# Delta rule loop: two steps a turn with buffers by parity, the late level first, and level copies shared by bank

## The reference

```python
m = jnp.einsum('bhnid,bhnjd->bhnij', kb, k) * dec_strict      # gram product, decayed
a = m + jnp.eye(CHUNK)
u = triangular_solve(a, v * beta)                             # the inverse of a is needed
w = triangular_solve(a, kb * exp(gam))
qk = jnp.einsum('bhnid,bhnjd->bhnij', q, k) * dec_incl
def step(s, xs):                                              # from chunk to chunk
    v_new = u_c - w_c @ s
    o = qd_c @ s + qk_c @ v_new
    s = gl_c * s + kd_c.T @ v_new
```

## Time and profile before

| | |
|---|---|
| median of 3 runs | 3768.53 us (3765.59 to 3772.26) |
| profiled execution, its own time | 3773.59 us |
| its span | 3771.8 us |
| mean granted clock of TensorE | 0.935 |
| PE, PEld | 3270.4 us (87%), 2736.9 us (73%) |
| DVE, ACT, POOL | 1995.1 (53%), 1669.3 (44%), 1715.4 (45%) |
| delta rule stage | about 1062 to 1702 us of the span |

### The profile page before, as it was taken

The page is one execution under the profiler, slowest core; times in us unless marked ns, Lnnn a source line. Parts: engine busy times, 40 slices in busy tenths (PEclk is TensorE's granted clock), DMA queues, the critical chain, the costliest instruction groups (busy, mean ns, idle before and its releaser), DMA issues. The chain is left out here.

```text
span 3771.8 us, 114554 instructions
## 1 busy us (share of the span) xinstructions
PE 3270.4 (87%) x49145; PEld 2736.9 (73%) x49145; DVE 1995.1 (53%) x2896; ACT 1669.3 (44%) x2453; POOL 1715.4 (45%) x1364
## 2 busy tenths in 40 slices
PE   6899999999968788775677566999999999999998
PEld 3677888888857777764666535878877887787877
DVE  5488510111025555555666667665565546657575
ACT  5566422442135565552444424564454453323243
POOL 0211222333035555532666337546646656656564
PEclk8899999999979999995877867999999999999999
DMA  5133443353233333324433365766675666645453
GB/s 199 48 68 73 101 101 95 107 139 114 70 99 112 112 114 113 109 86 116 114 103 91 134 211 183 234 228 197 199 249 173 204 204 248 245 161 220 177 223 123
DMA packets 438348, 555.94 MB, mean 147 GB/s; under 512 B 119788, under 2 KB 355664, under 8 KB 413656
## 3 DMA queue, kind: packets, MB, share of 16 engines
q1 hardware_dynamic: 411936, 514.10, 42.7%
q10 hardware_dynamic: 20536, 21.58, 1.7%
q0 software_dynamic: 5632, 16.78, 1.5%
HBM read 354.42 MB, written 197.97 MB: 146 GB/s over the span
## 5 line engine op out<-in xcount | busy, mean ns | idle before, releaser
L3015 PE MATMUL o_pg<-o_t_hi,o_s_hi 128*128 128x512 f32 x2016 | 793.4, 394 | 47.1 <-ACT o_part L3062 13.0
L3017 PE MATMUL o_pg<-o_t_lo,o_s_hi 128*128 128x512 f32 x2016 | 790.2, 392 | 0.0
L3018 PE MATMUL o_pg<-o_t_hi,o_s_lo 128*128 128x512 f32 x2016 | 789.9, 392 | 0.0
L600 PE MATMUL p_pg<-h_hi,p_whi 128*128 128x512 f32 (+1 forms) x1384 | 531.6, 384 | 9.5 <-DVE p_wlo L827 9.5
L600 PE MATMUL p_pg<-h_lo,p_whi 128*128 128x512 f32 (+1 forms) x1384 | 519.4, 375 | 0.0
L600 PE MATMUL p_pg<-h_hi,p_wlo 128*128 128x512 f32 (+1 forms) x1384 | 519.3, 375 | 0.0
L3015 PEld LDWEIGHTS o_pg<-o_t_hi,o_s_hi 128*128 128x128 f32 x2016 | 381.8, 189 | 137.7 <-DVE o_s_lo L3222 35.7
L3018 PEld LDWEIGHTS o_pg<-o_t_hi,o_s_lo 128*128 128x128 f32 x2016 | 381.9, 189 | 80.1
L3017 PEld LDWEIGHTS o_pg<-o_t_lo,o_s_hi 128*128 128x128 f32 x2016 | 381.7, 189 | 78.7
L3222 DVE TENSOR_TENSOR o_s_lo<-o_raw,o_s_hi 128x512 fp32r<-128x512 f32 x288 | 267.5, 931 | 202.6 <-ACT o_s_hi L3051 202.6
L600 PEld LDWEIGHTS p_pg<-h_hi,p_whi 128*128 128x128 f32 x1384 | 262.4, 190 | 61.0 <-DVE p_wlo L827 9.8
(11 more groups left out here) (334 smaller groups left out, 6669.3 us busy)
## 6 DMA issues: line engine op xcount, KB each, us to landing
o_raw<-in_w_mlp SPq DMA_DIRECT2D x32, 1024.0 KB, 6.4
scr_f<-o_xf SPq DMA_DIRECT2D x64, 512.0 KB, 8.1
o_raw<-scr_f SPq DMA_DIRECT2D x32, 1024.0 KB, 5.3
scr_w<-o_pre SPq DMA_DIRECT2D x16, 1792.0 KB, 7.1
o_t_raw<-scr_w SPq DMA_DIRECT2D x28, 1024.0 KB, 4.9
g_kqvb<-scr_kqv SPq DMA_DIRECT2D x72, 384.0 KB, 3.5
o_xf<-scr_x SPq DMA_DIRECT2D x22, 1024.0 KB, 7.7
p_raw<-in_w_in SPq DMA_DIRECT2D x38, 512.0 KB, 5.8
```

The lines of the kernel that those rows point to most:

```text
L600: last = nc.tensor.matmul(pg[0:m, bank, 0:n], w[:, q, k, 0:m], h[bank][:, k, :], start=(k == 0 and j == 0), stop=(k == KT - 1 and j == 2))
L3015: nc.tensor.matmul(out, s_hi[:, q, k, :], t_hi[:, q, k, :], start=(not more and k == 0), stop=False, skip_group_check=more)
L3017: nc.tensor.matmul(out, s_hi[:, q, k, :], t_lo[:, q, k, :], start=False, stop=False, skip_group_check=more)
L3018: last = nc.tensor.matmul(out, s_lo[:, q, k, :], t_hi[:, q, k, :], start=False, stop=(k == 3), skip_group_check=more)
```

## The change

- `steps`: body 0 and body 1 written out, a loop of 16 turns with bodies 2 and 3, then bodies 34, 35 and 36 written out. `at`, `chunks` and the column slices count two steps a turn.
- `nn`, `tt`, `am` and `kqvb` are pairs of buffers, chosen by the parity of the chunk. The copies `hand_nn`, `hand_tt`, `keep_inverse` and `vtake` go, with `nn2`, `tt2`, `ttb` and `vt`. `residual_end` reads the turned values from PSUM.
- `take(l)` on ACT copies bank 0 alone; a new `take_rest(l)` on DVE copies bank 1; PE waits for both.
- The order within a body changes on PE, ACT, DVE and POOL; SP loads the rows of gamma two chunks ahead and `kqvb` first.

The core of the diff:

```diff
-    return n0 * per + c if i is None else i * per + (n0 * per + c)
+    return n0 * per + c if i is None else i * (2 * per) + (n0 * per + c)
...
-        nn, nn2, tt, tt2, ttb, am, amb = (sb("g_" + n, [P, *W]) for n in ("nn", "nn2", "tt", "tt2", "ttb", "am", "amb"))
+        nn, tt, am = ([sb(f"g_{n}{p}", [P, *W]) for p in range(2)] for n in ("nn", "tt", "am"))
+        amb = sb("g_amb", [P, *W])
...
             body(None, 0, True, False, True)
-            with eng.Fori(0, NCH - 2) as i:
-                body(i, 1, True, True, True)
+            body(None, 1, True, True, True)
+            with eng.Fori(0, (NCH - 4) // 2) as i:
+                body(i, 2, True, True, True)
+                body(i, 3, True, True, True)
+            body(None, NCH - 2, True, True, True)
             body(None, NCH - 1, True, True, False)
...
                 def body(i, n, a, c, pre):          # SP
+                    if a:
+                        if i is not None or n > 1:
+                            sp.wait_ge(qs_done, at(i, n, 1, -1))
+                        load_kqvb(i, n)
                     if pre:
-                        sp.wait_ge(d_ready, at(i, n, 1, 1))
-                        load_rows(i, n + 1)
+                        if i is not None or n < NCH - 2:
+                            sp.wait_ge(d_ready, at(i, n, 1, 2))
+                            load_rows(i, n + 2)
                         sp.wait_ge(kkq_done, at(i, n, 1, 1))
                         load_kqa(i, n + 1)
-                    if a:
-                        if c:
-                            sp.wait_ge(qs_done, at(i, n, 1, 0))
-                        load_kqvb(i, n)
...
                     def grown(l):
                         pe.wait_ge(tx_ready, at(i, n, 3, l + 1))
+                        pe.wait_ge(tx_rest, at(i, n, 3, l + 1))
...
                     def ks():
+                        pe.wait_ge(kqvb_in, at(i, m, 32, 32))
+                        pe.wait_ge(s_ready, at(i, m, 1, 1))
                         pe.wait_ge(o_ready, at(i, m, 1, 1))
...
                     def qs():
-                        pe.wait_ge(vt_ready, at(i, m, 1, 1))
+                        pe.wait_ge(z_ready, at(i, m, 1, 1))
...
                     def take(l):                    # ACT
                         act.wait_ge(tx_done, at(i, n, 3, l + 1))
-                        nc.scalar.activation(txs[:, :, :, :, :], pa[:, :, :, :, :], ACT.Copy).then_inc(tx_ready, 1)
+                        nc.scalar.activation(txs[:, 0], pa[:, 0], ACT.Copy).then_inc(tx_ready, 1)
...
+                    def take_rest(l):               # DVE
+                        dve.wait_ge(tx_done, at(i, n, 3, l + 1))
+                        dve.tensor_copy(txs[:, 1], pa[:, 1]).then_inc(tx_rest, 1)
...
                     def decay():
-                        if c:
-                            dve.wait_ge(tt2_ready, at(i, n, 1, 0))
+                        if i is not None or n > 1:
+                            dve.wait_ge(tz_done, at(i, n, 1, -1))
...
                     def residual_end():
                         dve.wait_ge(z_half, at(i, m, 1, 1))
-                        dve.wait_ge(vt_ready, at(i, m, 1, 1))
-                        dve.tensor_tensor(z[:, :, :, :], z[:, :, :, :], vt[:, :, :, :], ALU.subtract).then_inc(z_ready, 1)
+                        dve.wait_ge(kv_turned, at(i, m, 1, 1))
+                        dve.tensor_tensor(heads_first(z), heads_first(z), pd[:, :, 1], ALU.subtract).then_inc(z_ready, 1)
```

More of the change, by code:

```diff
@@ L945, in phase_gdn @@
         glq = sb("g_glq", [P, NCH, 2 * PAIRS])
-        kqa, kqvb = sb("g_kqa", [P, 2, 2, PAIRS, CH]), sb("g_kqvb", [P, 2, 3, PAIRS, CH])
+        kqa = sb("g_kqa", [P, 2, 2, PAIRS, CH])
+        kqvb = [sb(f"g_kqvb{p}", [P, 2, 3, PAIRS, CH]) for p in range(2)]
         grow = sb("g_grow", [P, *W])
@@ L1031, in load_kqvb @@
                         src = e.skqv[:, ds(chunks(i, n)[g], 1)]
-                        sp.dma_start(kqvb[:, g].rearrange("p (c j) a t -> p c (j a t)", c=1),
+                        sp.dma_start(kqvb[n % 2][:, g].rearrange("p (c j) a t -> p c (j a t)", c=1),
                                      src.rearrange("p c j t -> p c (j t)")).then_inc(kqvb_in, 16)
@@ L1191, in product @@
                         pe.sem_inc(go, 1)
-                        turn(side(pa, 1), tile(tt))
-                        to_channels(side(pa, 0), tile(nn), tile(tt)).then_inc(tx_done, 1)
+                        turn(side(pa, 1), tile(tt[p]))
+                        to_channels(side(pa, 0), tile(nn[p]), tile(tt[p])).then_inc(tx_done, 1)
                     def grown(l):
                         pe.wait_ge(tx_ready, at(i, n, 3, l + 1))
+                        pe.wait_ge(tx_rest, at(i, n, 3, l + 1))
                         pe.sem_inc(go, 1)
@@ L1203, in late_product @@
                         pe.wait_ge(pred2_done, at(i, m, 3, l - 2))
-                        pe.wait_ge(nn2_ready, at(i, m, 1, 1))
                         pe.sem_inc(go, 1)
-                        turn(side(pc, 1), tile(tt2))
-                        to_channels(side(pc, 0), tile(nn2), tile(tt2)).then_inc(tx2_done, 1)
+                        turn(side(pc, 1), tile(tt[q]))
+                        to_channels(side(pc, 0), tile(nn[q]), tile(tt[q])).then_inc(tx2_done, 1)
                     def late_grown(l):
@@ L1253, in amvn @@
                         back(side(pb, 0), tile(amb), tile(vn)).then_inc(amvn_done, 1)
+                    if c:
+                        late_grown(2)
                     if a:
@@ L1257, in body @@
                     if c:
-                        kv()
-                        late_grown(2)
-                        late_product(3)
+                        late_product(3)
+                        ks()
+                        kv()
+                        late_grown(3)
                     if a:
                         product(0)
-                    if c:
[L1264 to L1267, removed]
                     if c:
@@ L1271, in body @@
                     if a:
-                        product(1)
+                        grown(0)
                     if c:
@@ L1275, in body @@
                     if a:
-                        grown(1)
+                        product(1)
                     if c:
@@ L1279, in body @@
                     if a:
+                        grown(1)
+                    if c:
+                        kdvn()
+                    if a:
                         product(2)
                     if c:
-                        kdvn()
                         amvn()
@@ L1333, in keep_am @@
                             act.wait_ge(amvn_done, at(i, m, 1, 0))
[L1334 to L1356, removed]
+                        src = am[m % 2]
+                        nc.scalar.activation(amb[:, :, 0:2, :], src[:, :, 0:2, :], ACT.Copy)
+                        nc.scalar.activation(amb[halves(1), :, 2:4, :], src[halves(0), :, 2:4, :], ACT.Copy)
+                        nc.scalar.activation(amb[halves(0), :, 2:4, :], src[halves(1), :, 2:4, :], ACT.Copy).then_inc(amb_ready, 1)
                     def vntake():
@@ L1388, in gaps @@
                 def gaps(i, n):
-                    nc.gpsimd.tensor_copy(cola[:, :, :, :].unsqueeze(2), colq[:, 0:3, ds(i + n if i is not None else n, 1)])\
+                    nc.gpsimd.tensor_copy(cola[:, :, :, :].unsqueeze(2), colq[:, 0:3, ds(i * 2 + n if i is not None else n, 1)])\
                         .then_inc(cola_ready, 1)
@@ L1407, in take_colb @@
                 def take_colb(i, n):
-                    st = i + n if i is not None else n
+                    st = i * 2 + n if i is not None else n
                     nc.gpsimd.tensor_copy(colb[:, :, :, :].unsqueeze(2), colq[:, Q_KDEC:Q_REST, ds(st, 1)])
@@ L1422, in body @@
                     m = n - 1
+                    if pre:
+                        gaps(i, n + 1)
+                    if a:
+                        pool.wait_ge(tt_half, at(i, n, 1, 1))
+                        pool.wait_ge(c_ready, at(i, n, 1, 1))
+                        nc.gpsimd.tensor_tensor(tt[n % 2][:, :, :, :], tt[n % 2][:, :, :, :], c2[:, :, :, :], ALU.add).then_inc(tt_init, 1)
+                    if pre:
+                        pool.wait_ge(tt_init, at(i, n, 1, 1))
+                        seeds(i, n + 1)
                     if c:
@@ L1533, in body @@
                     if a:
+                        decay()
                         attend()
                     if c:
+                        residual()
+                        late_block(3)
+                    if a:
+                        take_rest(0)
+                    if c:
                         keys()
-                        late_block(3)
-                        residual()
+                        residual_end()
                     if a:
@@ L1541, in body @@
                     if c:
-                        residual_end()
+                        late_block(4)
                         carried()
```

(3 more changed lines are left out.)

79 lines of the change are left out of this document (30 added, 49 removed).

## The result

The changed kernel takes 4170.0 us (median of four executions), against 3770.4 us for the one before: a ratio of 1.105, 95% interval 1.102 to 1.108. The profiled execution took 4175.8 us, its span is 4174.0 us.

What follows compares the result with a forecast made beforehand. No engine was full; the two-step body's code loading on PE was to set the pace. Sixteen turns of 859 us plus 50 us for two written-out steps replace 563.1: +346 us, 4115 us, range 3965 to 4290.

Steps and rivals of the forecast that it cites:

- The mechanism: Delta rule loop on PE: the two-step body does not stay and is loaded again every turn; chance 0.80.
- The pace: PE's code loading in the delta rule loop: one block every 4.13 us, averaged over eight intervals between stalls.
- Blocks of a turn: PE's two-step loop body: 13 blocks loaded a turn, 53.7 us, sixteen turns 859 us.
- The two steps newly written out: Steps 1 and 34 on PE run first-time code: 25 us each, 50 us together.
- The jump: PE's loop end: the jump back may wait behind an unneeded load; in the upper bound, 14 blocks at 4.6 us.
- The most that any row shows PE to keep is 8 blocks: PE's code: 8 blocks loaded for the present loop, against 12.4 for the two-step body, taken as not staying.
- The new order: PE's queue in a delta rule step: reordering and sharing worth 0 to 0.3 us a step, nothing under the load pace.
- SyncE and POOL ... both ends zero: Gamma rows loaded a step ahead and POOL's distances first: PE waits for neither queue, so zero gain.
- set at what it was: residual_end on DVE, reading PSUM instead of vt: its time taken as unchanged.
- the order pays: Rival: code stays, three copies each reach PE 0.42 us sooner, 1.26 us a step, 3748 us; chance 0.11.

Runs made afterwards that it cites:

- e1: The kernel before with a turn of two steps and nothing else changed: 4133.2 us, ratio 1.096.
- e3: The changed kernel with PE's 37 bodies written out and no jump on PE, other engines keeping their loops: 4050.5 us, ratio 1.074.
- e8: The kernel before with the first half of each gram product computed ten times, a body of 8.5 blocks: 4456 us in one execution.
- e10: The kernel before with the first half of each gram product computed three times, a body of 6.7 blocks: 4049 us in one execution.
- e11: The kernel before with the first half of each gram product computed twice, a body of 6.45 blocks: 3779 us in one execution.
- e2: The changed kernel with one step a turn, its handover between buffers left out so only the time counts: 3754.2 us, ratio 0.995.
- e5: The changed kernel with one step a turn, ScalarE's two handover copies back, single am and kqvb: 3760.4 us, ratio 0.997.
- e6: e5 with the three level copies whole on ScalarE, none shared: 3756.1 us, ratio 0.996.
- e7: The kernel before with the three level copies shared by bank, old order, one step a turn: 3765.7 us, ratio 0.997.

## Why the prediction was right

*The mechanism* was right: the two-step body is loaded in every turn, e1 shows it alone. Forecast 400 blocks, 408 measured.

*The pace* of 4.13 us a block, read from eight stalls of code that ran first, was right: 4.11. That it agrees so closely is in part luck, for the pace isn't one number: 3.92 in e1's loop (222 blocks in 870.1 us), 4.11 in e3, 3.65 in e8.

*Blocks of a turn* was the term that was mis-sized: 13 forecast, 13.9 measured, 223 - 208 = 15 blocks more in the sixteen turns. 15 x 4.11 = 62 us, less 3 for the pace. The two steps newly written out took 21.1 (1098.20 to 1119.28) and 24.4 us (2036.78 to 2061.13) instead of 25 each, -5. Together +54, which is the difference between the forecast +346 and the +400 of the profiled execution. The jump, whose price the forecast had only in its upper bound, has its part in it: e3.

*"The most that any row shows PE to keep is 8 blocks"* was right in its direction and wrong as a size. It misreads: 2 of those 8 blocks were loaded from 1086 to 1097.85 us, during body 0 and before the loop's first gram product, so the row shows at most some 6 blocks for the body that stays. And e10 shows that a body of 6.7 no longer stays. The Trainium skill ("Advanced Engine Details and Errata", section ISA Cache) names 128 KB for TensorE in lines of 256 instructions, which makes 8 lines. The runs agree with the line (127 matmuls between stalls) and allow the 8 only with about a line and a half that the body can't use: nothing here shows what occupies it. The Trainium skill ("Runtime: NRT & Kernel Launch", section Instruction fetch mechanics) says that a taken branch to code outside the two pages held must wait for its load. The trace agrees with the wait, 4.72 us at 1234.48, but not with two pages: a body of 6.45 blocks stayed (e11).

*The new order* was underrated: 0 to 0.3 us a step forecast, 0.59 measured (e2). The waits that I counted are there: for `z` 0.9 us, forecast 1.1 less the 0.2 that the list leaves out, and for the copies 0.4, forecast 0.6 less 0.2. The gap is in the kernel before, and the step that failed is *"SyncE and POOL ... both ends zero"*. The old order's step varies from 16.1 to 16.8 us, that of e2 is 15.8 every time (15.6 to 15.9). The trace of the kernel before shows why, first in its waits from 1150 to 1660 us, then in a long step (16.83 us) and in a short one (16.07):

```profile
POOL g_dd L1395 <- DMA g_grow<-scr_gam: 119.2, 31, 4.3
```

```profile
1341.22 1.04 POOL L1395 TENSOR_TENSOR g_dd<-g_grow,g_cola 128x512 f32<-128x512 f32 x1 [4.29 <-DMA g_grow<-scr_gam]
...
1342.30 0.63 ACT L1290 ACTIVATE g_dd<-g_dd 128x512 f32<-128x512 f32 x1 [2.08 <-POOL g_dd L1395]
...
1345.02 0.69 PE L1077 MATMUL g_pc<-g_txs 64*64 64x64 f32 x32 [1.36 <-ACT g_txs L1328]
...
1619.42 1.04 POOL L1395 TENSOR_TENSOR g_dd<-g_grow,g_cola 128x512 f32<-128x512 f32 x1 [3.52 <-DMA g_grow<-scr_gam]
...
1620.50 0.63 ACT L1290 ACTIVATE g_dd<-g_dd 128x512 f32<-128x512 f32 x1 [1.31 <-POOL g_dd L1395]
...
1623.22 0.69 PE L1077 MATMUL g_pc<-g_txs 64*64 64x64 f32 x32 [0.59 <-ACT g_txs L1328]
```

POOL waits for gamma's rows, ACT waits for POOL, and in ACT's queue the copy of the late product of level 4 stands behind that, so PE waits too. In steps 3 to 33 the step less PE's waits for late copies is 14.84 to 14.88 us: what varies is this chain. It stands in the largest line of the earlier trace rows, 47.6 us in 62 waits, which the prediction put down to ACT's copies: one wait a step is always 0.62 us, the other, this one, goes from 0.59 to 1.36. The new order loads the rows two chunks ahead, and in e2, e5 and e6 POOL no longer waits for them; in e7, the old order, it still does (108.4 us in 28 steps). No run moves that load alone, so how much of the 0.59 us is its, and how much the rest of the order's, stays open.

`residual_end`, set at what it was, got 0.44 us shorter. Before, it takes 670 to 1568 ns, in 29 of 36 steps over 900, each time with POOL's operations beside it; afterwards, with one input in PSUM, 675 to 679. The longest one before, and one of e2:

```profile
1538.33 1.04 POOL L1398 TENSOR_TENSOR g_c<-g_msk,g_cola 128x512 f32<-128x512 f32 x1
1538.36 1.57 DVE L1512 TENSOR_TENSOR g_z<-g_z,g_vt 128x512 f32<-128x512 f32 x1
...
1539.34 1.49 POOL L1399 TENSOR_TENSOR g_c<-g_msk,g_cola 128x512 f32<-128x512 f32 x1
...
1413.16 0.68 DVE L1501 TENSOR_TENSOR g_z<-g_z,g_pd 128x512 f32<-128x512 f32 x1
1413.18 1.28 POOL L1391 TENSOR_TENSOR g_ei<-g_ee,g_msk 128x512 f32<-128x512 f32 x1
```

The first ends only 0.59 us after POOL's next operation began, which in turn takes 1.49 us instead of 1.04; the second runs beside POOL undisturbed. `vt` lay in SBUF, so dropping it took this collision away.

*The rival "the order pays"* had its point of decision at 0.57 us a step, and 0.59 were measured: by the prediction's own sum, had the code stayed, the change would have come out about even, because three more steps run first-time code. Its reason was wrong, though. It took ACT's copies for 64.0 of the 93.0 us waited, but 47.6 of these are the late copies, which the change doesn't share; the shared ones are the 16.4. Sharing alone gave 0.25 us a step (e7), not 1.26.

*Left open:* the 35 us between e1 and the changed kernel, both with 408 blocks. The traces show only where they lie: a block of the loop comes every 3.92 us in e1 and every 4.11 in the changed kernel, and from 1200 to 1900 us PE waits 215.8 and 237.3 us for "issue", in fewer steps. No run takes the parts of the change one by one in a two-step turn.

## What to carry to other kernels

Count the instructions of a hardware loop's body on each engine before making it longer: unrolling by two cost 360 us by itself (e1), since here a block of 256 instructions came every 3.9 to 4.1 us and was issued in only 1.9. The number to read is the packets of the instruction queue on the page, and waits for "issue" in the middle of a group of equal matmuls. When work is shared out to a second engine, look at what stands behind it in that engine's queue: of three shared copies two were worth 0.63 us a step, and the third took back more than that. And follow a wait through the queues: PE's wait for a copy by ACT began with a DMA of rows that POOL needed.

## What the runs showed of the hardware that I had not expected

- PE's code stayed at 6.45 blocks of 256 instructions and not at 6.7 (e11, e10).
- Just above the limit, the code was loaded around every second turn only: 9 blocks in two turns at 6.7 and at 7.2 blocks, 24.9 and 25.1 us a step; 10 in every turn at 8.5 (e8).
- A jump back to code that is not held kept PE waiting for 4.5 to 5.2 us (4.7 to 5.2 in 12 turns of the changed kernel, 4.51 in e1, 4.75 and 4.93 in e10).
- An operation of DVE with both inputs in SBUF took up to 1568 ns beside POOL's operations, and 679 and 691 ns in the two steps where POOL ran nothing beside it; with one input in PSUM it took 675 to 679 ns either way.
